# Sparse attention's key selection: query tile 5 counted on ScalarE, level correction and masks built inside the attention

## The reference

```
dots = einsum('bthd,bsd->bths', qi, ki)
score = einsum('bths,bth->bts', relu(dots), wi * IDX_SCALE)
score = where(admissible, score, -inf)          # keys below the end of the query's 64-chunk
_, sel = top_k(score, n_sel)                    # n_sel = 256 for the prompt
logits = q.k_sel / 8 - slope * |q_pos - sel|    # 16 heads on 4 key heads, ALiBi
out = softmax(logits) @ v_sel
```

## Time and profile before

| | us |
|---|---|
| median of 3 runs | 3404.48 |
| profiled execution | 3402.7 |
| its span | 3400.9 |
| PE busy | 3134.8 (92%) |
| DVE busy | 1513.2 (44%) |
| POOL busy | 1042.6 (31%) |
| ACT busy | 887.1 (26%) |

### The profile page before, as it was taken

The page is one execution under the profiler, slowest core; times in us unless marked ns, Lnnn a source line. Parts: engine busy times, 40 slices in busy tenths (PEclk is TensorE's granted clock), DMA queues, the critical chain, the costliest instruction groups (busy, mean ns, idle before and its releaser), DMA issues.

```text
span 3400.9 us, 49928 instructions
## 1 busy us (share of the span) xinstructions
PE 3134.8 (92%) x19621; PEld 2921.1 (86%) x19621; DVE 1513.2 (44%) x2880; ACT 887.1 (26%) x1921; POOL 1042.6 (31%) x504
## 2 busy tenths in 40 slices
PE   7896999976999999999968999987889999999996
PEld 7586777764999999999967999976689999999996
DVE  2589764432434333432352555563334343334335
ACT  2355444423110111101122445453311101110112
POOL 2132000032443334333443222213244433443333
PEclk8998799988999999999988999998989999999997
DMA  2121000011211111111112111111021111111111
GB/s 82 32 51 51 1 1 1 1 56 36 65 45 62 37 43 43 55 44 43 44 47 68 55 41 46 47 39 56 21 75 50 44 56 37 44 48 56 37 49 51
DMA packets 209355, 149.48 MB, mean 44 GB/s; under 512 B 28914, under 2 KB 195764, under 8 KB 209236
## 3 DMA queue, kind: packets, MB, share of 16 engines
q1 hardware_dynamic: 209236, 147.85, 14.2%
HBM read 128.09 MB, written 19.73 MB: 43 GB/s over the span
## 4 chain that ended last, share of the span: by engine, by line
PE 84%; DVE 7%; ACT 3%; issue 2%; POOL 1%; DMA 1%; ACTq 0%; SPq 0%; POOLq 0%; DVEq 0%
PE psum L151 46%; PE psum L1901 15%; PE psum L1522 5%; PE psum L612 4%; PE psum L578 2%; PE psum L593 2%; DVE junk L827 2%; PE psum L1186 2%; PE psum L1160 2%; PE psum L1174 1%; PE psum L533 1%; PE psum L547 1%; ACT x_newA L1574 1%; DVE ln_part L1769 1%; ACT x_newB L1574 1%
## 5 line engine op out<-in xcount | busy, mean ns | idle before, releaser
L151 PE MATMUL psum<-x_hi,w_hi 128*128 128x352 f32 (+1 forms) x3192 | 1040.6, 326 | 29.5 <-POOL w_lo L122 13.8
L151 PE MATMUL psum<-x_lo,w_hi 128*128 128x352 f32 (+1 forms) x3192 | 1028.1, 322 | 0.0
L151 PE MATMUL psum<-x_hi,w_lo 128*128 128x352 f32 (+1 forms) x3192 | 1028.0, 322 | 0.0
L120 POOL TENSOR_TENSOR w_hi<-w_raw,zeros 128x1024 fp32r<-128x1024 f32 (+1 forms) x209 | 386.8, 1851 | 1615.4 <-PE psum L151 1359.2
L151 PEld LDWEIGHTS psum<-x_hi,w_hi 128*128 128x128 f32 (+1 forms) x3192 | 601.8, 189 | 31.6 <-issue 21.2
L151 PEld LDWEIGHTS psum<-x_lo,w_hi 128*128 128x128 f32 (+1 forms) x3192 | 602.9, 189 | 0.4
L151 PEld LDWEIGHTS psum<-x_hi,w_lo 128*128 128x128 f32 (+1 forms) x3192 | 601.6, 188 | 0.5
L122 POOL TENSOR_TENSOR w_lo<-w_raw,w_hi 128x1024 fp32r<-128x1024 f32 (+1 forms) x209 | 485.1, 2321 | 16.4
L1973 DVE TENSOR_TENSOR gate<-psum,gate 128x352 f32<-128x352 f32 x132 | 69.3, 525 | 830.5 <-PE psum L151 830.5
L1901 PE MATMUL psum<-h_hi,w_hi 128*128 128x352 f32 x1056 | 340.6, 323 | 0.0
L1901 PE MATMUL psum<-h_lo,w_hi 128*128 128x352 f32 x1056 | 338.3, 320 | 0.0
(11 more groups left out here) (458 smaller groups left out, 4166.9 us busy)
## 6 DMA issues: line engine op xcount, KB each, us to landing
w_raw<-in_ffn_w_dram SPq DMA_DIRECT2D x132, 512.0 KB
w_raw<-in_b_w_in_dram SPq DMA_DIRECT2D x24, 512.0 KB
w_raw<-in_ple_w_gate_dram SPq DMA_DIRECT2D x16, 512.0 KB
x_nat<-in_x_prompt_dram SPq DMA_DIRECT2D x8, 512.0 KB, 3.7
w_raw<-in_a_w_in_dram SPq DMA_DIRECT2D x8, 512.0 KB
w_raw<-in_a_w_in_dram SPq DMA_DIRECT2D x16, 256.0 KB
x_rows<-x_rows SPq DMA_DIRECT2D x8, 512.0 KB, 2.6
out_new_b_v_prompt_dram<-valsB SPq DMA_DIRECT2D x8, 512.0 KB, 3.4
```

The source lines that it names most:

```text
L120: nc.gpsimd.tensor_tensor(c.w_hi[s][:, 0:kc], c.w_raw[s][:, 0:kc], zero, ALU.add).then_inc(c.split[s], 1)
L151: last = c.nc.tensor.matmul(out, w, x, start=(n == 0), stop=(n == 3 * len(terms) - 1))
```

## The change

ScalarE's share of the search becomes tiles 5, 6 and 7, VectorE's tiles 2, 3 and 4. After the 31 rounds only the sign of ACT's levels and a clean-up of tiny levels remain ahead of the attention. The level correction becomes a generator `settle` of five pieces, run behind the mask of tile 4. The masks are made two tiles ahead instead of three, so that the mask of tile 2 is made during tile 0, and two pieces are issued per step instead of one; leftover pieces run at the tile's start. The recount of the correction writes to `tie` in place of `junk`.

```diff
-    ON_ACT = (6, 7)
-    ON_DVE = (2, 3, 4, 5)
+    ON_ACT = (5, 6, 7)
+    ON_DVE = (2, 3, 4)
+    NA, ND = len(ON_ACT), len(ON_DVE)
...
-            v.wait_ge(s_signs, 4 + 2 * b + 2)
+            v.wait_ge(s_signs, 2 * NA + NA * b + NA)
...
-        nc.vector.tensor_scalar(level[:, 4:6], level[:, 4:6], -1.0, None, ALU.mult).then_inc(s_top, 1)
+        nc.vector.tensor_scalar(level[:, ND:6], level[:, ND:6], -1.0, None, ALU.mult).then_inc(s_top, 1)
...
-        nc.vector.tensor_scalar(above[:, 4:6], level[:, 4:6], 1.25 * 2.0 ** -24, None, ALU.mult).then_inc(s_top, 1)
...
-        for t in ON_ACT:
-            nc.vector.tensor_scalar(junk[t][:, :], score(t), above[:, t - 2:t - 1], 0.0, ALU.is_ge,
-                                    ALU.add, accum_out=count[:, t - 2:t - 1]).then_inc(s_top, 1)
...
+        def settle():
...
+            nc.vector.tensor_scalar(above[:, a], level[:, a], 1.25 * 2.0 ** -24, None, ALU.mult).then_inc(s_mask, 1)
+            v.wait_ge(s_mask, masks + 1)
+            nc.vector.tensor_tensor(above[:, a], above[:, a], level[:, a], ALU.add).then_inc(s_mask, 1)
+            masks += 2
+            yield
+            for t in ON_ACT:
+                v.wait_ge(s_mask, masks)
+                nc.vector.tensor_scalar(tie[:, 0:keys_of(t)], score(t), above[:, t - 2:t - 1], 0.0, ALU.is_ge,
+                                        ALU.add, accum_out=count[:, t - 2:t - 1]).then_inc(s_mask, 1)
+                masks += 1
+                yield
...
+            nc.vector.tensor_tensor(level[:, a], above[:, a], level[:, a], ALU.max).then_inc(s_mask, 1)
+            masks += 3
+            yield
...
-        masks = 0
-        for _ in masking(2):
-            pass
-        later = None
+        later = ()
         for g in range(STEPS + 3):
             if g % 8 == 0 and g < STEPS:
                 t = g // 8
-                later = masking(t + 3) if t + 3 < QT else mask_sample() if t + 3 == SAMPLE else None
+                for _ in later:
+                    pass
+                if t + 2 <= SAMPLE:
+                    later = itertools.chain(masking(t + 2) if t + 2 < QT else mask_sample(), settle() if t == 2 else ())
...
             if g < STEPS:
                 read_logits(g, 1)
-                if later is not None:
-                    next(later, None)
+                for _ in itertools.islice(later, 2):
+                    pass
```

More of the change, by code:

```diff
@@ L1 @@
+import itertools
 import math
@@ L731, in scalar @@
             if b == 0:
-                act.wait_ge(s_signs, 4)
+                act.wait_ge(s_signs, 2 * NA)
             for t in ON_ACT:
@@ L791, in vector @@
                 rows(*ROWS_AFTER[subs[i]])
-        nc.vector.memset(level[:, 0:4], 2.0).then_inc(s_top, 1)
-        nc.vector.memset(level[:, 4:6], -2.0).then_inc(s_top, 1)
+        nc.vector.memset(level[:, 0:ND], 2.0).then_inc(s_top, 1)
+        nc.vector.memset(level[:, ND:6], -2.0).then_inc(s_top, 1)
         done += 2
@@ L799, in vector @@
                                     accum_out=count[:, t - 2:t - 1]).then_inc(s_top, 1)
-        done += 4
+        done += ND
         v.wait_ge(s_top, done)
-        nc.vector.tensor_scalar(above[:, 0:4], count[:, 0:4], float(TOPK), None, ALU.is_ge).then_inc(s_top, 1)
-        v.wait_ge(s_signs, 2)
+        nc.vector.tensor_scalar(above[:, 0:ND], count[:, 0:ND], float(TOPK), None, ALU.is_ge).then_inc(s_top, 1)
+        v.wait_ge(s_signs, NA)
         for t in ON_ACT:
@@ L806, in vector @@
                                     ALU.is_ge).then_inc(s_top, 1)
-        done += 3
+        done += 1 + NA
         v.wait_ge(s_top, done)
@@ L855, in vector @@
[L855 to L863, removed]
+                                       op1=ALU.mult).then_inc(s_mask, 1)
@@ L864, in vector @@
+        masks = 1
         for j in (0, 1):
             v.wait_ge(s_kout[j], 48)
+        def settle():
+            nonlocal masks
+            a = slice(ND, 6)
+            v.wait_ge(s_mask, masks)
[5 more added lines that the diff above has]
+            for t in ON_ACT:
+                v.wait_ge(s_mask, masks)
+                nc.vector.tensor_scalar(tie[:, 0:keys_of(t)], score(t), above[:, t - 2:t - 1], 0.0, ALU.is_ge,
+                                        ALU.add, accum_out=count[:, t - 2:t - 1]).then_inc(s_mask, 1)
+                masks += 1
+                yield
+            v.wait_ge(s_mask, masks)
+            nc.vector.tensor_tensor(missed[:, a], count[:, a], wanted[:, a], ALU.is_ge).then_inc(s_mask, 1)
+            v.wait_ge(s_mask, masks + 1)
+            nc.vector.tensor_tensor(above[:, a], above[:, a], missed[:, a], ALU.mult).then_inc(s_mask, 1)
+            v.wait_ge(s_mask, masks + 2)
+            nc.vector.tensor_tensor(level[:, a], above[:, a], level[:, a], ALU.max).then_inc(s_mask, 1)
+            masks += 3
+            yield
```

2 lines of the change are left out of this document (removed).

## The result

| | before | after |
|---|---|---|
| median of 7 runs each, us | 3404.37 (3397.68 to 3405.16) | 3413.83 (3407.72 to 3419.17) |
| profiled execution, us (its span) | 3402.7 (3400.9) | 3413.83 (3412.1) |
| the 31 rounds, us | 128.99 | 142.27 |
| first sign count to first reading, us | 142.99 | 148.12 |
| half clock ends, us behind the first reading | 36.9 | 54.8 |

The ratio after/before is 1.0036 [1.0027, 1.0046]: 0.36% slower, more than a measurement of this kernel leaves open, and just above the range of the prediction.

The account below looks back on a forecast made before the run. The prediction took DVE's search to set the pace until the first reading and PE the attention behind it. First reading -3.0 and attention +2.5 gave -0.5 us, put at 3403.5 us, range 3394 to 3413.

Parts of the forecast that it names:

- The likeliest case, no change: Whole kernel: 3403.5 us, a difference too small to measure; chance 0.62.
- Three of the prediction's own signs of being wrong: Search and attention: stall sum beyond 20 us, tile 2 outside 24 to 27, half clock ending over 7 off 379.6.
- The round: Each search round becomes ACT-bound at 3.87 us instead of 3.66, costing +6.5 us over 31 rounds (+5 to +8).
- V's drains: Four rounds in which ACT also copies rows of V end later, +1.1 us.
- Ahead of the rounds: ACT signs and flips three tiles instead of two before the rounds, +0.6 us (0 to +1.5).
- Behind them: Between rounds and attention, the correction and tile 2's mask go away, -7.7 us.
- POOL's splits: In the rounds, nine split pairs delay the small operations 1.3 us each, 12 against 15.5: -3.5 us (-15.5 to +13).
- rival (a): In the rounds, POOL's pairs start earlier and hold the level update longer: 3.2 us each, 3420 us; chance 0.10.
- First reading: At the attention's start, DVE reads the first logits 3.0 us sooner, near 339.4.
- The packing: In the attention, the added mask and correction work on DVE makes PE wait, +2.5 us (0 to +6).
- a rival (c): In the attention, TensorE's full clock returns some steps sooner, worth about 6 us, giving 3396; chance 0.12.
- Rival (d): In the rounds, stalls vanish (3392 us) or the round follows DVE's shorter counts (3374); chance 0.08.

Follow-up runs that it names:

- the small splits: POOL splits only the first 128 of 1024 columns of units 3 to 11: changed kernel 3395.97 us (0.9978), kernel before 3396.09 (0.9973).
- the clock raised at the same step: 24 unused dense matmuls ahead of attention step 9: in the kernel before 3401.64 us, in the changed kernel 3409.4.
- the masks alone: Kernel before with correction and all masks inside the attention, tiles 6 and 7 still on ScalarE: 3403.78 us (1.000); run once more, 3402.2.
- the balanced version alone: Changed kernel with tiles 3, 4, 5 on ScalarE and 2, 6, 7 on VectorE, correction behind tile 2's mask, no unused matmuls: 3404.12 us (0.9995).
- the kernel with the gap filled: Kernel before with 185 unused matmuls on TensorE between its last projection and the first reading: 3405.93 us (1.0008).

## Why the prediction was wrong

The likeliest case, no change, didn't come; the time is 0.8 us above the range. Three of the prediction's own signs of being wrong showed: the stalls passed 20 us (20.1), tile 2 took 28.2 us where 24 to 27 were given, and the half clock ended 21 us behind 379.6. By its own steps:

- **The round.** Right: ACT-bound, 3.89 us for 3.87, the hand-over 0.10 where 0.05 was taken (bounds 0 and 0.1); +7.3 us for +6.5. V's drains +0.4 for +1.1. Ahead of the rounds: from the first count to ACT's first round 6.46 us for 5.87, +0.6 as forecast. Behind them -7.7 as forecast.
- **POOL's splits: the step that failed, and the term that was mis-sized.** Forecast -3.5, measured +4.7 (20.1 against 15.4), inside its bounds of -15.5 to +13. The step held that PE waits for ACT's drains and so locks to the round, with all nine pairs alike. That holds for five pairs, at 1.1 us each. For the first four PE waits for no drain of a piece: it comes late from its two stops for V's rows and goes on at its own pace, so POOL starts 3.0 to 3.2 us into the round, just ahead of `missed`, and each pair makes its round 3.4 to 3.8 us longer. That is read from traces of after; no run moves PE's stops alone. This is rival (a)'s mechanism in four of nine cases, with a mean of 2.2 us per pair, just over the 2.1 named as its point of decision. Against (a) the prediction held that only one pair in nine did it before; there were two, that of the earlier trace rows and one at 263.31 and 264.34, where `missed` took 0.79 and `level` 2.25 us. That the splits are the cause of the stalls is shown by the small splits. The Trainium skill, "SBUF — State Buffer", section "SBUF: two separate sides", has the rule of the exclusive lock that the prediction quoted; the trace agrees (`missed` ends at 228.37 and `level` at 230.86, just behind splits that end at 228.35 and 230.82).
- **First reading.** -3.0 forecast; -3.0 + 8.2 for the stalls + 0.8 for the round - 0.7 for the drains, with 0.2 or less for the rest, is the measured +5.1.
- **The packing.** +2.5 forecast; with the clock raised at the same step tiles 2 and 3 are 2.0 and 0.6 longer, tile 0 0.3. Right.
- **The clock.** The prediction held the half clock's length fixed and made an earlier return a rival (c); a later return was not among the cases. It lasted 55 us instead of 37, worth 5.4 us in tile 1 and about 4.1 - 2.0 = 2 in tile 2. In the medians less of it is seen: after is 7.8 us slower than before with the clock raised alike, and 9.5 to 12.5 without, so the clock adds some 2 to 5. Shown is that the clock falls without PE's long gap and that one program takes both lengths; what decides the length is open.
- **Rival (d).** Its 3374 takes 31 x 0.95 off the forecast, but 0.95 is the distance to the round before; from the forecast's 3.87 us it is 1.16, 36 us. Nothing else hangs on it.

The sum, by the pair with the clock raised alike: search +4.7, packing +2.9 with tile 0, together 7.6 of the 7.8 us between the medians. Had only the stalls been sized rightly, the forecast would have been 8.2 us higher, 3411.7: slower, and still inside the range. The last 2 us to the measured time are of the size of the clock's share.

What stays open: why the masks alone, and the balanced version alone, reach the end of the attention some 5 us sooner and show none of it in the median. The clock's low stretches in later stages differ from execution to execution (42 to 57 us of them between 700 and 1000), enough to hide that much, but no run ties the two together.

## What to carry to other kernels

Two engines that meet in every round are balanced by the sum of each with its hand-over: moving one more count here took DVE's 3.05 us down to 2.1 and put ACT's at 3.2, so the round grew; another deal of the same six counts gave 3.53. Small operations behind a hand-over can be held by another engine's long ones, here POOL's splits: work out the phase of each pair, not of an average one, and read which engine sets it. And a comparison of stages should hold the TensorE clock alike, by a short stretch of dense matmuls at the same step, before a difference of a few us is put down to the code; and the granted clock has to be looked at again, since in one of four kernels here it fell once more.

## What the hardware did unexpectedly

PE was busy for 54.59 of 54.70 us, all but the last 0.5 at 1.2 GHz (granted 0.50), and in the kernel with the gap filled it fell from 2.4 GHz (1.00 until 343) to 1.2 by 344 and stayed there, busy for 51.91 of 52.00 us. With 24 unused matmuls ahead of step 9 the full level was back 21 to 23 us behind the first reading. The Trainium skill, "TensorE: Matmul & The Clock Gate", "Part 1: The HAM clock gate", says that the clock is set by how busy the PE has lately been; the busy time of these rows alone doesn't explain their clock, and the measurement decides.

Behind a split on POOL, DVE operations of six columns took up to 2.25 us instead of 0.17, those with one tensor input too (1.75 at L834 of before), while the counts in the same stretches kept their durations (means 0.61, 0.74 and 0.88 for 384, 512 and 640 columns in after's rounds).
